# Delta-rule chunks: block inverse put on the right-hand side, then forward substitution by 32 rows in four column groups

## What is computed

```
gcum = cumsum(gc); decay = exp(where(incl, gcum[:, None] - gcum[None, :], -inf))
lhs = eye + where(strict, bc[:, None] * (kc @ kc.T) * decay, 0)
rhs = [vc * bc, kc * bc * exp(gcum)]
sol = triangular_solve(lhs, rhs, lower=True, unit_diagonal=True)
u = sol[:, :DV] - sol[:, DV:] @ S
o = (qc * exp(gcum)) @ S + (qc @ kc.T * decay) @ u
S = S * exp(gcum[-1]) + (kc * exp(gcum[-1] - gcum)).T @ u
```

## Time and profile before

| | us |
|---|---|
| median of 3 runs | 2688.94 |
| lowest, highest | 2684.39, 2692.87 |
| profiled execution | 2684.61 |
| its span, first to last instruction | 2682.8 |
| PE busy | 2507.8 (93%) |
| DVE busy | 1007.8 (38%) |
| ACT busy | 707.6 (26%) |
| DeltaNet chunks, first L1015 to the end of the last chunk | about 244 to 615 |
| one prompt chunk, from its L1015 at 411.81 to the next one's at 450.97 | 39.16 |

### The profile page before, as it was taken

How to read it: one execution, slowest core, us unless ns; L and a number is a source line. 1 busy time by engine, 2 the same in 40 slices (tenths; PEclk the granted TensorE clock), 3 DMA queues, 4 the chain that set the end, 5 groups by cost and what they waited for, 6 DMA issues and landing times.

```text
span 2682.8 us, 39175 instructions
## 1 busy us (share of the span) xinstructions
PE 2507.8 (93%) x16348; PEld 1558.3 (58%) x16348; DVE 1007.8 (38%) x1782; ACT 707.6 (26%) x1251; POOL 64.3 (2%) x66
## 2 busy tenths in 40 slices
PE   6998999999999999999999999999997899989994
PEld 3555888885555566555555556765455444434443
DVE  4356455452223055552332548722245001101115
ACT  3132222221111111120243046731024122222224
POOL 0000000000000000000000000000000000000003
PEclk9999999999999999999999999999997999999998
DMA  7000212204000111141003011131306556657436
GB/s 314 32 32 35 75 44 107 75 31 159 32 32 32 35 52 61 65 156 72 32 18 151 32 38 40 40 116 67 109 23 267 222 208 269 233 231 284 176 129 228
DMA packets 65269, 291.99 MB, mean 109 GB/s; under 512 B 8956, under 2 KB 32068, under 8 KB 44612
## 3 DMA queue, kind: packets, MB, share of 16 engines
q1 hardware_dynamic: 52996, 255.92, 25.2%
q0 software_dynamic: 8928, 22.03, 2.4%
q10 hardware_dynamic: 3168, 11.54, 1.1%
HBM read 694.20 MB, written 56.63 MB: 280 GB/s over the span
## 4 chain that ended last, share of the span: by engine, by line
PE 80%; DMA 7%; DVE 6%; ACT 4%; issue 2%; SPq 1%; POOL 0%; DVEq 0%; ACTq 0%; POOLq 0%
PE psum L531 30%; PE psum L675 16%; PE psum L1519 8%; DMA arena<-in_moe 6%; PE psum L1377 4%; PE psum L1503 4%; PE psum L1102 3%; PE psum L630 2%; ACT arena L1758 1%; PE psum L560 1%; PE psum L1090 1%; PE psum L1015 1%; PE psum L991 1%; PE psum L1488 1%; PE psum L1082 1%
## 5 line engine op out<-in xcount | busy, mean ns | idle before, releaser
L531 PE MATMUL psum<-arena 128*128 128x384 f32 x2544 | 826.6, 487 | 10.9 <-DVEq L330 6.1
L531 PEld LDWEIGHTS psum<-arena 128*128 128x128 f32 x2544 | 483.0, 190 | 352.7 <-issue 10.2
L675 PE MATMUL psum<-arena 128*128 128x384 f32 (+1 forms) x1920 | 537.1, 425 | 6.4 <-ACT arena L689 3.3
L675 PEld LDWEIGHTS psum<-arena 128*128 128x128 f32 x1920 | 339.6, 191 | 152.9 <-ACT arena L689 4.5
L1519 PE MATMUL psum<-arena 128*32 128x256 f32 x5632 | 325.4, 387 | 34.2 <-DMA arena<-in_moe 33.0
L1519 PEld LDWEIGHTS psum<-arena 128*32 128x32 f32 x5632 | 178.8, 112 | 167.0 <-DMA arena<-in_moe 39.0
L1503 PE MATMUL psum<-arena 128*32 128x512 f32 x1408 | 160.5, 594 | 9.9 <-DMA arena<-in_moe 9.2
L1927 ACT ACTIVATE arena<-psum 32x512 f32<-32x512 f32 x174 | 102.2, 588 | 226.9 <-PE psum L1503 225.3
L1377 PE MATMUL psum<-arena 128*128 128x512 f32 (+1 forms) x384 | 126.0, 487 | 0.3 <-issue 0.3
L2623 DVE TENSOR_TENSOR arena<-arena,psum 128x256 f32<-128x256 f32 x44 | 18.5, 421 | 280.7 <-PE psum L1519 190.2
L689 ACT ACTIVATE arena<-psum 128x384 f32<-128x384 f32 x96 | 46.6, 489 | 274.6 <-PE psum L675 214.2
(11 more groups left out here) (541 smaller groups left out, 2402.7 us busy)
## 6 DMA issues: line engine op xcount, KB each, us to landing
arena<-in_moe SPq DMA_DIRECT2D x532, 1024.0 KB
arena<-in_ada SPq DMA_DIRECT2D x12, 2048.0 KB, 9.3
gate_raw<-arena SPq DMA_DIRECT2D x96, 192.0 KB, 1.8
arena<-gate_raw SPq DMA_DIRECT2D x8, 2304.0 KB, 8.4
y_rows<-arena ACTq DMA_DIRECT2D x22, 512.0 KB
arena<-in_gate SPq DMA_DIRECT2D x5, 2048.0 KB, 8.6
arena<-in_br SPq DMA_DIRECT2D x4, 2048.0 KB, 8.1
arena<-in_qkv SPq DMA_DIRECT2D x3, 2048.0 KB, 16.2
```

The costliest lines, as they stand in the source:

```text
L531: last = nc.tensor.matmul(pset(s)[:, n, :], w[:, kk, :], src[:, kk, n * N3:(n + 1) * N3], start=(kk == 0), stop=(kk == K - 1))
L675: last = nc.tensor.matmul(bank(6 + u % 2)[:, cols * p:cols * (p + 1)], w[:, m % 4, kk, :], HT[:, kk, n * N3 + cols * p:n * N3 + cols * (p ...
```

## The change

For the eight prompt chunks the last stage (`SOLVE = 3`, blocks of 32 to 128 rows) no longer builds the inverse. With X the inverse of the diagonal blocks of 32 rows and P = X L (only what lies below those blocks), `(I + P) u = X cVB`. So the new code:

- turns L instead of X: the masked L^T of stage 3 (cLK1) is transposed on PE inside stage 2, behind its first step, and ACT copies it into cLK0;
- computes X cVB at once (4 matmuls into bank 4, ACT copies them to cU) and P^T (4 matmuls); DVE evicts these as I - P^T into cPS;
- solves by forward substitution: three steps, each for the next 32 rows of all four heads. A step is 4 matmuls of 32 weight columns and 128 columns of data, one per head, each in its own column group, into one bank. DVE copies heads 0 and 1, ACT heads 2 and 3, as 32x128 blocks into the rows of cU;
- has no further product: PE goes on to the output once the last rows are in cU.

The table gives 17 instead of 13 fill matmuls at `start` of a prompt chunk, none at stage 2's first step, 2 behind `right3` and the first two steps of the solve, none at `w` and `o`. The sum of a prompt chunk stays 40. The sample chunk keeps its old code and its old counts.

The diff, cut to its core:

```
-        counts = [("start", 13), ("ops", 4)]
+        counts = [("start", 13 if last else 17), ("ops", 4)]
         for st, steps in enumerate(STEPS[c], 1):
-            counts += [("turn%d" % st, 2), ("right%d" % st, 1)] + [("step%d_%d" % (st, i), 1) for i in range(steps - (st == len(STEPS[c])))]
-        counts += [("w", 2), ("o", 2)]
+            if st == SOLVE:
+                counts += [("right%d" % st, 2)] + [("step%d_%d" % (st, i), 2) for i in range(steps - 1)]
+                continue
+            counts += [("turn%d" % st, 2), ("right%d" % st, 1)]
+            counts += [("step%d_%d" % (st, i), 1) for i in range(st == SOLVE - 1 and not last, steps - (last and st == len(STEPS[c])))]
+        counts += [("w", 2), ("o", 2)] if last else [("w", 0), ("o", 0)]
...
+                    if lv == SOLVE:
+                        pe.wait_ge(c_xt, 2 * (n + 1) + 3 * c)
+                        for f in range(2):
+                            pe.wait_ge(c_x, 2 * at - 1 + f)
+                            for h in (2 * f, 2 * f + 1):
+                                last = nc.tensor.matmul(bank(4)[:, hs[h]], gXT[h], cVB[:, hs[h]], start=True, stop=True)
+                        last.then_inc(c_u, 1)
+                        for f in range(2):
+                            for e in range(2):
+                                last = nc.tensor.matmul(bank(5 * f)[:, hs[e]], cLK0[:, hs[2 * f + e]], gXT[2 * f + e],
+                                                        start=True, stop=True)
+                            last.then_inc(c_p, 1)
+                        fill(c, "right%d" % lv)
+                        pe.wait_ge(c_us, c + 1)
+                        pe.wait_ge(c_ps, 2 * n + 2)
+                        for i in range(steps):
+                            if i:
+                                pe.wait_ge(c_x, 2 * (at + i))
+                                pe.wait_ge(c_xt, 2 * (n + 1) + 3 * c + i)
+                            for h in range(GH):
+                                o = h * P + 32 * (i + 1)
+                                last = nc.tensor.matmul(bank(1 + i % 2)[32 * h:32 * h + 32, 0:P], cPS[:, o:o + 32], cU[:, hs[h]],
+                                                        start=True, stop=True)
+                            last.then_inc(c_d, 2)
+                            if i < steps - 1:
+                                fill(c, "step%d_%d" % (lv, i))
+                        continue
...
+                        if lv == SOLVE - 1 and not sample and i == 0:
+                            pe.wait_ge(c_lk, n + 2)
+                            for f in range(2):
+                                for e in range(2):
+                                    last = nc.tensor.transpose(bank(3 + f)[:, hs[e]], cLK[SOLVE % 2][:, hs[2 * f + e]], ident)
+                                last.then_inc(c_t, 1)
...
+                    fill(c, "o")
+                    pe.wait_ge(c_x, 2 * (STEP0[c][-1] + STEPS[c][-1]))
+                    pe.wait_ge(c_xt, 2 * STAGE0[c + 1] + 3 * (c + 1))
...
+                    if lv == SOLVE:
+                        act.wait_ge(c_u, c + 1)
+                        nc.scalar.activation(cU, bank(4), ACT.Copy).then_inc(c_us, 1)
+                        evict(c, "right%d" % lv)
+                        for i in range(steps):
+                            act.wait_ge(c_d, 2 * (STEP0[c][lv - 1] + i + 1))
+                            for h in (2, 3):
+                                last = nc.scalar.activation(cU[32 * (i + 1):32 * (i + 2), h * P:(h + 1) * P],
+                                                            bank(1 + i % 2)[32 * h:32 * h + 32, 0:P], ACT.Copy)
+                            last.then_inc(c_xt, 1)
+                            if i < steps - 1:
+                                evict(c, "step%d_%d" % (lv, i))
+                        continue
...
+                    if lv == SOLVE:
+                        for f in range(2):
+                            dve.wait_ge(c_p, 2 * (STAGE0[c] + lv - 1) + 1 + f)
+                            tt(hd(cPS[:, 256 * f:256 * (f + 1)], 2), by(ident, 2), hd(bank(5 * f)[:, 0:256], 2),
+                               ALU.subtract).then_inc(c_ps, 1)
+                        for i in range(steps):
+                            dve.wait_ge(c_d, 2 * (STEP0[c][lv - 1] + i + 1))
+                            for h in (0, 1):
+                                nc.vector.tensor_copy(cU[32 * (i + 1):32 * (i + 2), h * P:(h + 1) * P],
+                                                      bank(1 + i % 2)[32 * h:32 * h + 32, 0:P]).then_inc(c_x, 1)
+                        continue
```

More of the change, by code:

```diff
@@ L134 @@
 STEPS = [[3, 3, 3]] * 8 + [[3, 1]]
+SOLVE = 3
 STAGE0 = [sum(len(s) for s in STEPS[:c]) for c in range(NT)]
@@ L1086, in _ @@
                     for f in range(2):
-                        pe.wait_ge(c_xt, 2 * n + 1 + f)
+                        pe.wait_ge(c_xt, 2 * n + 3 * c + 1 + f)
                         for e in range(2):
@@ L1116, in _ @@
                 fill(c, "w")
-                pe.wait_ge(c_x, 2 * (STEP0[c][-1] + STEPS[c][-1]))
                 if not sample:
@@ L1120, in _ @@
                     ada_rows(pe, 0, AWL)
-                for h, a in enumerate(hs):
-                    last = nc.tensor.matmul(bank(4)[:, a], gXT[h], cVB[:, a], start=True, stop=True)
-                last.then_inc(c_u, 1)
-                fill(c, "o")
-                pe.wait_ge(c_us, c + 1)
+                    fill(c, "o")
+                    pe.wait_ge(c_x, 2 * (STEP0[c][-1] + STEPS[c][-1]))
+                    pe.wait_ge(c_xt, 2 * STAGE0[c + 1] + 3 * (c + 1))
+                else:
+                    pe.wait_ge(c_x, 2 * (STEP0[c][-1] + STEPS[c][-1]))
+                    for h, a in enumerate(hs):
+                        last = nc.tensor.matmul(bank(4)[:, a], gXT[h], cVB[:, a], start=True, stop=True)
+                    last.then_inc(c_u, 1)
+                    fill(c, "o")
+                    pe.wait_ge(c_us, c + 1)
                 if not sample:
@@ L1633, in _ @@
                     for i in range(steps):
+                        if lv == SOLVE - 1 and not sample and i == 0:
+                            for f in range(2):
+                                act.wait_ge(c_t, 2 * n + 3 + f)
+                                nc.scalar.activation(cLK0[:, 256 * f:256 * (f + 1)], bank(3 + f)[:, 0:256], ACT.Copy).then_inc(c_xt, 1)
                         if (c, "step%d_%d" % (lv, i)) in GDN_COUNT:
@@ L1642, in _ @@
                     nc.scalar.activation(cPS, bank(2), ACT.Copy)
-                act.wait_ge(c_u, c + 1)
-                nc.scalar.activation(cU, bank(4), ACT.Copy).then_inc(c_us, 1)
+                    act.wait_ge(c_u, c + 1)
+                    nc.scalar.activation(cU, bank(4), ACT.Copy).then_inc(c_us, 1)
                 evict(c, "o")
```

## The result

| | before, us | after, us |
|---|---|---|
| median (4 runs each) | 2686.66 | 2661.61 |
| lowest to highest | 2678.22 to 2692.87 | 2659.03 to 2669.5 |
| profiled execution | 2684.61 | 2669.50 |
| a prompt chunk | 39.17 | 36.50 |

The ratio of the times is 0.9922, 95% interval 0.9905 to 0.9939: 21 us faster (16 to 25), where 20 were forecast; the medians of the table differ by 25, which the interval holds too. The profiled execution of after is the slowest of its four.

What follows compares the result with a forecast made beforehand. PE was taken as the bound; seven later prompt chunks at -2.45 us (-3.24 + 0.29 + 0.5) and the first at -2.95 made -20 us, from the median 2688.94 to 2669 us, range 2660 to 2683.

Steps and rivals of the forecast that it cites:

- What bounds the kernel: PE, busy 37.84 of 39.17 us in a prompt chunk, plus three waits: 0.38, 0.88 and a fifth of a microsecond.
- Prices: PE costs read from rows of before: step streaming 0.22 us, trip in and out of narrow matmuls 0.34, four transposes 0.62.
- Part 1: Last stage of a prompt chunk, up to the next chunk: from 14.80 us to 11.56, -3.24.
- Part 2: Stage 2 of a prompt chunk: four transposes (0.62 us) replace a fill matmul (0.33), +0.29.
- Part 3: Chunk opening: four more fill matmuls, 1.30 us, ahead of L1063; +0.5 us, wait ahead of L1082 stays about 0.8.
- Hand-overs: Copies behind P^T and the solve's steps stay hidden; behind a step data after 1.10 us, PE back after 1.11.
- Part 4: First chunk: extra fill at its start costs nothing, standing ahead of long waits; the chunk gains 2.95 us.
- (a): Solve's short steps cost more than streaming, each border 0.27 us; gain 6 to 13 us, about 2679; chance 0.16.
- (b): Chunk opening: delayed L1063 moves the whole DVE part by 1.3 us; gain 14, 2674 us; no separate chance given.
- (c): Behind the chunks: the next part waits for a load that comes no earlier; 2686 us; chance 0.05.
- (d): Solve: narrow steps drop PE's clock to 1.2 GHz for part of each chunk; slower, up to 2760 us; chance 0.05.
- What would show it: Trace: period 36.7 us, step's next row 0.35 later, no wait at steps or output, PE busy down 15, clock 1.00.

Runs made afterwards that it cites:

- experiment 3: Changed kernel with ada_rows cut in two halves in place of fill between the solve's steps; ratio to the kernel before 0.9912, period 35.53 us.
- Experiment 4: Changed kernel with 14 instead of 17 fill matmuls at start, 7 instead of 4 at ops; ratio to the kernel before 0.9929, period 36.02 us.
- experiment 7: Changed kernel with no fill between the solve's steps, 8 instead of 4 fill matmuls at ops; ratio to the kernel before 0.9946, period 36.82 us.
- the second comparison: Changed kernel unaltered, timed again beside the kernel before; ratio 0.9934, measured -17.7 us.
- experiments 2 and 12: Changed kernel with a fill table as near the old one as possible, timed twice; ratios to the kernel before 1.0016 and 1.0013.

## Why the prediction was right

**What bounds the kernel.** PE's work and three gaps. Right: the chunk fell by 2.67 us, PE's busy time in it by 2.08 and its idle time by 0.59.

**Prices.** A step 0.36 to the next row against 0.35, fill behind it 0.84 and 0.85 against 0.86 with both borders, the last step 0.24 and `ada_rows` 1.83 against 0.22 and 1.86 (the 0.10 for the way in, which the sum books on the last step, lies in the row of fill ahead of it). From the fill behind P^T to the output, 429.69 to 434.94, it is 5.25, exactly the sum. In these rows a trip costs 0.33, against 0.34; experiment 3, which saves two, gives 0.27.

**Part 1.** 427.84 to the next chunk at 439.46 is 11.62 us, against a sum of 11.56. Right; the 0.06 are X cVB, at 0.96 instead of 0.90.

**Part 2** is the term that was mis-sized: +0.29 forecast, +0.03 measured (415.47 to 427.84 is 12.37; before, 423.83 to 436.17, 12.34). The four transposes take 0.43 to 0.44 here:

```profile
424.95 0.60 PE L1141 MATMUL psum<-cst,arena 128*128 128x128 f32 x4
425.39 1.06 PE L1134 MATMUL psum<-arena 128*128 128x128 f32 x8
```

The 0.62 that I took from L1082's row held 0.2 of waiting for DVE's last subtraction, in the weight loads, which the rows of PE don't show and those of PEld do. In the kernel before:

```profile
414.85 0.60 PE L1051 MATMUL psum<-cst,arena 128*128 128x128 f32 x4
436.52 0.20 PEld L1082 LDWEIGHTS psum<-cst,arena 128*128 128x128 f32 x2 [0.21 <-DVE arena L2143]
```

A matmul row in a chain is not the price of the work alone; L1051, with the next group at 415.29, would have shown 0.44. With it the term would have been +0.11. The second step gives 0.07 of that back: it took 0.97 before (433.65 to 434.62) and takes 0.90 behind the transposes (425.39 to 426.29).

**Part 3.** The opening is 0.49 longer, forecast +0.5; the wait ahead of L1114 is 0.71, forecast 0.8. Experiment 4 takes the 0.5 back. With -3.18, +0.03 and +0.49 the three parts make -2.66, against -2.45.

**Hand-overs.** Hidden as forecast. The copies take 0.283 (0.29) and 0.270 (0.28), two in a row 0.59 on DVE (0.58). That agrees with the model of the Trainium skill that the prediction named ("VectorE: DVE Perf Modes", "Two Vector instructions with no wait between them"): the second head's copy, which starts in another quadrant, doesn't overlap the first, where L2125's four of 0.345 take 1.13 together. The hand-over's length is 1.18, not 1.10 (experiment 7).

**Part 4.** The first chunk's start to the second's went from 50.07 to 47.05: -3.02 against -2.95.

**Rivals.** (a) failed: the way out costs 0.12 (a step's 0.36 against 0.24 ahead of `ada_rows`) and the way in about 0.10, not 0.27. The Trainium skill, in "TensorEngine Tiling (Array Packing)", "Key Properties", says that a change of mode drains TensorE; the rows agree that a border is not free, at under half of the 0.27 of a full matmul instruction, and don't show what fills that time. (b) failed: 0.49, not 1.3. (c) failed in its mechanism, a wait for a load; part of the gain was lost further on, but by the clock. (d) failed: in chunks two to eight the clock is 1.00 throughout. But the clock did take some of the gain, elsewhere. The sum for the chunks (20.1 against 22.0) was 2 us low, by part 2 (seven times 0.26) and the 0.3 ahead of the eighth chunk, and the clock took about as much or more, so the total of 20 forecast meets 21 measured, and 17.7 in the second comparison, partly by these two cancelling.

**What would show it.** The period was put at 36.7 (36.50), and the signs for steps, opening and output came. One sign failed: PE's busy time over the program fell by 7 us, not 15. In the chunks it fell by 16.3, so outside them it rose by 9, which fits the lower clock of this execution (0.980 against 0.984): the same work is longer busy. The prediction had no term for the clock outside the chunks.

## What to carry to other kernels

Where one engine sets the pace and a dependency chain runs through it, shortening the chain gains little unless the independent work is dealt out anew: here, the column groups without the table, or the table without the column groups, gain 7 to 8 us each in the chunks where both together gain 22. Narrow matmuls in column groups pay most if they stand next to others of the same kind; a step of 0.22 us costs 0.56 between full matmuls, which is still less than the 0.89 of a full-width step. And take the price of an operation from a row in which it doesn't wait.

## What the runs showed of the hardware

A trip from full matmuls into four column groups and back costs about 0.3 us: 0.34 by the rows of before (0.10 ahead, 0.13 behind, 0.11 on the next group), 0.33 by those of after (0.36 for a step that streams 0.22, and 0.84 for 0.65 of fill), 0.27 by experiment 3.

PE's clock falls to 1.2 GHz for some microseconds behind waits as short as 0.37, 0.54 and 0.89 us within 5 us, in some executions and kernels and not in others with the same waits, at 1.7 us each; a wait of 2.87 us ahead of the last merge is followed by a loss of 3.0 or of nothing. The Trainium skill says, in "TensorE: Matmul & The Clock Gate", Part 1, that the monitor behind the gate runs freely and doesn't start with the kernel, so that the number of cold matmuls at one kernel's start varies from run to run. The two profiles of before, which drop at different places, agree. But the mean over runs differs between kernels too: 0.9788 and 0.9779 on two chips for the kernel of experiments 2 and 12, against 0.9815 to 0.9827 in five sets of runs of the kernel before. By the estimate above it lost 8 to 10 us by it, as much as or more than its chunks gained. For a change of 0.3% in this program the mean granted clock has to be read beside the time.
